# A split-precision matmul stream with high and low activations in one 512-column matmul

## The reference

```
proj = h @ w_in                      # 7 blocks of 128 columns a head: 3 q, 3 k, 1 v
g = g * sigmoid(g @ w_gate);  mix = g @ w_out        # state-space layer
a = h @ w_up
a = conv_b + sum(conv_w[j] * shifted(a, j))          # along time, width 3
ffn = (silu(gate) * up) @ w_down
x = x + g1 * mix;   x = x + g2 * ffn
```

## Time and profile before

| | |
|---|---|
| median of three runs | 2,897.93 us |
| the profiled execution | 2,893.69 us |
| its span, first to last instruction | 2,891.9 us |
| PE busy / DVE busy / ACT busy | 2,787.8 / 2,165.3 / 1,233.9 us |
| mean granted TensorE clock | 0.987 |
| mean DMA rate | 251 GB/s |

### The profile page before, as it was taken

One profiled execution on the slowest core, in us unless ns is written; L12 is line 12 of the kernel. 1 busy time (PEld: TensorE's weight loads), 2 busy tenths in 40 slices (PEclk: granted clock), 3 DMA queues, 4 the chain that ended last, 5 costly groups with the idle time before them and its releaser, 6 DMA issues.

```text
span 2891.9 us, 59942 instructions
## 1 busy us (share of the span) xinstructions
PE 2787.8 (96%) x23900; PEld 2730.2 (94%) x23900; DVE 2165.3 (75%) x2765; ACT 1233.9 (43%) x1687; POOL 458.6 (16%) x469
## 2 busy tenths in 40 slices
PE   8799999999989999999999999989989999999998
PEld 3789999999989999999999998989989999999998
DVE  7877766667759988889888778987688654566654
ACT  1434444444433544434444334444354443444532
POOL 4051101011024011000110121234311110011111
PEclk9999999999999999999999999999999999999999
DMA  9889877778757788778888877868868666665663
GB/s 360 344 288 372 287 256 256 253 252 269 253 162 258 281 298 286 266 230 300 298 297 304 270 245 217 240 216 300 283 216 300 184 176 185 187 183 183 180 182 110
DMA packets 241712, 724.83 MB, mean 251 GB/s; under 512 B 50912, under 2 KB 59872, under 8 KB 240736
## 3 DMA queue, kind: packets, MB, share of 16 engines
q1 hardware_dynamic: 185184, 666.98, 68.7%
q10 hardware_dynamic: 56320, 54.93, 6.1%
HBM read 700.58 MB, written 25.43 MB: 251 GB/s over the span
## 4 chain that ended last, share of the span: by engine, by line
PE 87%; DVE 6%; DMA 3%; issue 2%; ACT 1%; POOL 1%; ACTq 1%; SPq 0%; DVEq 0%; POOLq 0%
PE proj L1749 27%; PE proj L1750 27%; PE proj L1751 27%; DVE acc L986 2%; PE pmisc L1773 1%; DMA raw<-in_w_in 1%; DMA ada<-in_ada_w 1%; PE ps L1828 1%; DVE w_lo L1077 1%; PE ps L1855 1%; PE proj L1828 1%; PE ps L1939 1%; DVE work L1039 0%; ACT w_hi L547 0%; ACTq L615 0%
## 5 line engine op out<-in xcount | busy, mean ns | idle before, releaser
L1077 DVE TENSOR_TENSOR w_lo<-raw,w_hi 128x1024 fp32r<-128x1024 f32 (+1 forms) x896 | 1112.4, 1243 | 609.8 <-ACT w_hi L547 604.3
L547 ACT ACTIVATE w_hi<-raw 128x1024 fp32r<-128x1024 f32 (+1 forms) x896 | 933.8, 1045 | 1423.6 <-PE proj L1751 1322.7
L1749 PE MATMUL proj<-h_hi,w_hi 128*128 128x256 f32 x5120 | 1471.8, 287 | 47.2 <-DVE h_lo L1032 13.2
L1750 PE MATMUL proj<-h_lo,w_hi 128*128 128x256 f32 x5120 | 1456.7, 285 | 0.0
L1751 PE MATMUL proj<-h_hi,w_lo 128*128 128x256 f32 x5120 | 1456.3, 284 | 0.0
L1749 PEld LDWEIGHTS proj<-h_hi,w_hi 128*128 128x128 f32 x5120 | 988.4, 193 | 59.4 <-issue 20.7
L1750 PEld LDWEIGHTS proj<-h_lo,w_hi 128*128 128x128 f32 x5120 | 990.0, 193 | 0.0
L1751 PEld LDWEIGHTS proj<-h_hi,w_lo 128*128 128x128 f32 x5120 | 989.5, 193 | 0.0
L1749 PE MATMUL proj<-a_hi,w_hi 128*128 128x256 f32 x1920 | 547.2, 285 | 10.0 <-DVE x L1381 6.6
L1750 PE MATMUL proj<-a_lo,w_hi 128*128 128x256 f32 x1920 | 545.7, 284 | 0.0
L1751 PE MATMUL proj<-a_hi,w_lo 128*128 128x256 f32 x1920 | 545.6, 284 | 0.0
(11 more groups left out here) (237 smaller groups left out, 1516.3 us busy)
## 6 DMA issues: line engine op xcount, KB each, us to landing
raw<-in_w_up SPq DMA_DIRECT2D x352, 512.0 KB, 5.7
ada<-in_ada_w SPq DMA_DIRECT2D x348, 512.0 KB, 5.5
raw<-in_w_in SPq DMA_DIRECT2D x224, 512.0 KB, 5.6
raw<-in_w_down SPq DMA_DIRECT2D x128, 448.0 KB, 3.8
raw<-in_w_down SPq DMA_DIRECT2D x64, 512.0 KB, 3.7
raw<-in_w_out SPq DMA_DIRECT2D x32, 512.0 KB, 4.7
raw<-in_ssm_w_in SPq DMA_DIRECT2D x32, 512.0 KB, 4.6
raw<-in_ssm_w_gate SPq DMA_DIRECT2D x32, 512.0 KB, 5.8
```

Source lines behind the costliest of these rows:

```text
L547: nc.scalar.activation(w_hi[:, j % LAG, 0:nk * P], raw[:, j % s.ring, 0:nk * P], ACT.Copy).then_inc(hi_ready, 1)
L1077: V.tensor_tensor(w_lo[:, j % LAG, 0:nk * P], raw[:, j % s.ring, 0:nk * P], w_hi[:, j % LAG, 0:nk * P].bitcast(F32), ALU.subtract).then_in ...
L1749: mm(o, w_hi[:, j % LAG, w], hi[:, k, :], start=(k == (k0 if held else 0)), stop=False)
L1750: mm(o, w_hi[:, j % LAG, w], lo[:, k, :], start=False, stop=False)
```

## The change

Nine streams are marked wide: qkv1, qkv, ssm_out and all of layer 1's feed-forward part. In them the moving operand of the high weights is the high and the low activations side by side, 512 columns; the bank's first half takes high x high (and, as before, low x high), its second half high x low. The high and low activations become one tensor with two halves. Who takes a block out adds the second half to the first:

- heads: ACT copies the second half to SBUF, and DVE adds the first half to it (`gather`, due with the copy);
- into the residual stream: DVE does its multiply and add twice, first for the second half, and waits in between for its own result;
- up-projections: ACT copies the second half to `whole` (`tail`), DVE adds the first (`join_halves`) and frees the bank; the taps read `whole`, one step later.

In a block's last k step the low weights come before the wide matmul. The stream up1a is now one pass of 20 blocks in place of two of 12, up1a_end has 24 blocks in place of 20, and the ada parts taken there are spread over both.

```
+WIDE = {"qkv1", "qkv", "ssm_out", "up1a", "up1a_end", "down1a", "up1b", "up1b_end", "down1b"}
-    add("up1a", 2, 12, two, ada=(1, 10, spread(16, 20, 4)), sum_due=24, take_due=27)
-    add("up1a_end", 1, 20, two)
+    add("up1a", 1, 20, two, ada=(1, 10, spread(16, 36)))
+    add("up1a_end", 1, 24, two, ada=(1, 11, spread(16, 36, 4)), sum_due=44, take_due=47)
...
-        a_hi, a_lo = sb("a_hi", [HALF, T], F32R), sb("a_lo", [HALF, T], F32R)
-        h_hi, h_lo = sb("h_hi", [KT, T], F32R), sb("h_lo", [KT, T], F32R)
+        a_hl, h_hl = sb("a_hl", [2, HALF, T], F32R), sb("h_hl", [2, KT, T], F32R)
+        a_hi, a_lo, h_hi, h_lo = a_hl[:, 0], a_hl[:, 1], h_hl[:, 0], h_hl[:, 1]
...
+                    if s.wide:
+                        nc.scalar.activation(dst, proj[(7 * hl + m) % 2][:, T:2 * T], ACT.Copy).then_inc(q_tail, 1)
+                        return
                     nc.scalar.activation(dst, proj[(7 * hl + m) % 2][:, 0:T], ACT.Copy).then_inc(block_out, 1)
...
+                def tail(pl, side):
+                    def f(i):
+                        pair = pair0 + i * (s.blocks // 2) + pl
+                        block_ready(s, i, 2 * pl + side)
+                        wait(act, conv2, 2 * (pair - first_wide_pair) + side - 1)
+                        nc.scalar.activation(whole[:, side, :], proj[side][:, T:2 * T], ACT.Copy).then_inc(up_tail, 1)
+                    return f
...
+                    for side in range(2) if s.wide else ():
+                        late.setdefault(4 * pl + 5 + 2 * side, []).append(tail(pl, side))
+                    late.setdefault(4 * pl + 5 + s.wide, []).append(tap2(pl, 0))
+                    late.setdefault(4 * pl + 7 + s.wide, []).append(tap2(pl, 1))
...
+            def gather(s, i0, hl, m):
+                def f(i):
+                    b = 7 * hl + m
+                    dst = v_t if m == 6 else qk[:, hl, m, :]
+                    dve.wait_ge(q_tail, 14 * (i + i0 - 1) + b + 1)
+                    V.tensor_tensor(dst, proj[b % 2][:, 0:T], dst, ALU.add).then_inc(block_out, 1)
+                return f
...
+                    for m in range(7) if s.wide else ():
+                        late.setdefault(14 * hl + 2 * m + 5, []).append(gather(s, i0, hl, m))
                     late.setdefault(14 * hl + 14 + 7, []).append(softmax(i0, hl))
...
+                        if s.wide:
+                            V.scalar_tensor_tensor(out=x[:, k, :], in0=proj[b % 2][:, T:2 * T], scalar=g, in1=x[:, k, :],
+                                                   op0=ALU.mult, op1=ALU.add).then_inc(tail_added, 1)
+                            dve.wait_ge(tail_added, tails_before(name) + k + 1)
                         V.scalar_tensor_tensor(out=x[:, k, :], in0=proj[b % 2][:, 0:T], scalar=g, in1=x[:, k, :],
                                                op0=ALU.mult, op1=ALU.add).then_inc(block_out, 1)
...
+                def join_halves(pl, side):
+                    def f(i):
+                        pair = pair0 + i * (s.blocks // 2) + pl
+                        dve.wait_ge(up_tail, 2 * (pair - first_wide_pair) + side + 1)
+                        V.tensor_tensor(whole[:, side, :], proj[side][:, 0:T], whole[:, side, :], ALU.add
+                                        ).then_inc(block_out, 1)
+                    return f
...
+                        if s.wide:
+                            late.setdefault(4 * pl + 5 + 2 * side, []).append(join_halves(pl, side))
+                        late.setdefault(4 * pl + 5 + 2 * side + s.wide, []).append(taps10(pl, side))
...
+                    both = proj[b % 2][:, :].rearrange("p (c t) -> p c t", c=2)
+                    hl = a_hl if hi is a_hi else h_hl
...
+                        end = last and k == k0 + nk - 1
+                        if s.wide:
+                            if end:
+                                mm(o, w_lo[:, j % LAG, w], hi[:, k, :], start=False, stop=False)
+                            ins = mm(both, w_hi[:, j % LAG, w], hl[:, :, k, :], start=(k == 0), stop=end)
+                            if not end:
+                                ins = mm(o, w_lo[:, j % LAG, w], hi[:, k, :], start=False, stop=False)
+                            continue
                         mm(o, w_hi[:, j % LAG, w], hi[:, k, :], start=(k == (k0 if held else 0)), stop=False)
                         mm(o, w_hi[:, j % LAG, w], lo[:, k, :], start=False, stop=False)
```

More of the change, by code:

```diff
@@ L56 @@
 ADA = 4
+WIDE = {"qkv1", "qkv", "ssm_out", "up1a", "up1a_end", "down1a", "up1b", "up1b_end",
+        "down1b"}
 CHUNK = 4
@@ L67, in __init__ @@
         self.name, self.ring, self.tight, self.slots, self.ada = name, ring, tight, slots, ada
+        self.wide = name in WIDE
         self.length = len(pieces)
@@ L276, in build @@
         conv, o = cut(work, 2400, 2, 2, T)
+        whole, _ = cut(work, 5472, 2, T)
         silu, o = cut(work, o, 2, T)
@@ L392, in build, with tails_before @@
         UPS = {"up0a": 0, "up0a_end": 18, "up0b": 22, "up0b_end": 40,
-               "up1a": 44, "up1a_end": 56, "up1b": 66, "up1b_end": 86}
+               "up1a": 44, "up1a_end": 54, "up1b": 66, "up1b_end": 86}
+        first_wide_pair = min([UPS[n] for n in UPS if n in WIDE])
+        def tails_before(name):
+            n = 0
+            for s in st.values():
+                if s.name == name:
+                    return n
+                if s.wide and not s.name.startswith(("up", "qkv")):
+                    n += s.count * s.blocks
         def ada_part_done(name):
@@ L785, in f @@
                         fb = f0 + i * (s.blocks // 2) + pl
-                        block_ready(s, i, 2 * pl + side)
+                        if s.wide:
+                            act.wait_ge(block_out, s.block(i, 2 * pl + side) + 1)
+                        else:
+                            block_ready(s, i, 2 * pl + side)
                         wait(act, gated_ready, pair - 1)
-                        nc.scalar.activation(conv[:, pl % 2, side, :], proj[side][:, 0:T], ACT.Identity,
+                        nc.scalar.activation(conv[:, pl % 2, side, :], whole[:, side, :] if s.wide else proj[side][:, 0:T],
+                                             ACT.Identity,
                                              bias=tap_b[:, fb, side:side + 1],
@@ L791, in f @@
                         if side == 1:
-                            act.wait_ge(block_out, s.block(i, 2 * pl) + 1)
+                            if s.wide:
+                                act.wait_ge(conv2, 2 * (pair - first_wide_pair) + 1)
+                            else:
+                                act.wait_ge(block_out, s.block(i, 2 * pl) + 1)
                             nc.scalar.activation(silu[:, pl % 2, :], conv[:, pl % 2, 0, :], ACT.Silu).then_inc(silu_ready, 1)
@@ L1413, in f @@
                         dve.wait_ge(conv0, 2 * pair + side + 1)
-                        V.scalar_tensor_tensor(out=cv[:, 1:T], in0=proj[side][:, 0:T - 1], scalar=tap(1), in1=cv[:, 1:T],
+                        src, made = (whole[:, side], conv2) if s.wide else (proj[side], block_out)
+                        V.scalar_tensor_tensor(out=cv[:, 1:T], in0=src[:, 0:T - 1], scalar=tap(1), in1=cv[:, 1:T],
                                                op0=ALU.mult, op1=ALU.add).then_inc(conv1, 1)
                         dve.wait_ge(conv1, 2 * pair + side + 1)
-                        V.scalar_tensor_tensor(out=cv[:, 2:T], in0=proj[side][:, 0:T - 2], scalar=tap(0), in1=cv[:, 2:T],
-                                               op0=ALU.mult, op1=ALU.add).then_inc(block_out, 1)
+                        V.scalar_tensor_tensor(out=cv[:, 2:T], in0=src[:, 0:T - 2], scalar=tap(0), in1=cv[:, 2:T],
+                                               op0=ALU.mult, op1=ALU.add).then_inc(made, 1)
                         if side == 1:
-                            dve.wait_ge(block_out, s.block(i, 2 * pl + 1) + 1)
+                            if s.wide:
+                                dve.wait_ge(conv2, 2 * (pair - first_wide_pair) + 2)
+                            else:
+                                dve.wait_ge(block_out, s.block(i, 2 * pl + 1) + 1)
                             dve.wait_ge(silu_ready, pair + 1)
@@ L1426, in up @@
                     for side in range(2):
-                        late.setdefault(4 * pl + 5 + 2 * side, []).append(taps10(pl, side))
+                        if s.wide:
+                            late.setdefault(4 * pl + 5 + 2 * side, []).append(join_halves(pl, side))
+                        late.setdefault(4 * pl + 5 + 2 * side + s.wide, []).append(taps10(pl, side))
                 take_parts(s, late)
@@ L1748, in piece @@
                         w = slice((k - k0) * P, (k - k0 + 1) * P)
+                        end = last and k == k0 + nk - 1
+                        if s.wide:
+                            if end:
[4 more added lines that the diff above has]
+                            continue
```

(2 more changed lines are left out.)

8 lines of the change are left out of this document (4 added, 4 removed).

## The result

| | before | after |
|---|---|---|
| median of four runs | 2,899.23 us (2,894.52 to 2,902.14) | 2,873.57 us (2,867.78 to 2,876.29) |
| span of the profiled execution | 2,891.9 us | 2,873.1 us |
| mean granted TensorE clock | 0.987 | 0.985 |

The ratio is 0.9911, 95% interval 0.9895 to 0.9926: 26 us faster. The forecast was 86 us faster and a range of 2,790 to 2,858 us; the time lies above it. The sign was right, the size was not.

What follows compares the result with a forecast made beforehand. PE's matmul stream was taken as the bound, its pitch set by the next weights' load. Terms -94.5 + 1.3 + 3.5 + 3.4 + 0.5 + 1 - 1 = -85.8 gave 2,807.9, forecast 2,812 us, range 2,790 to 2,858.

Steps and rivals of the forecast that it cites:

- the term of PE: Wide streams: one weight load of three goes, a k step takes 0.336 instead of 0.360 us; 94.5 us saved.
- extra time goes with every matmul: Rival, wide streams: 13 ns belong to each change of weights, a step takes 347 ns; 2,856 us, chance 0.13.
- The reading of the earlier trace: Steady matmul stream: the next weights' load, about 120 ns and not following the array's clock, sets the 256-column pitch.
- K steps, instruction counts: Wide streams: 3,936 k steps, each with three 256-column matmuls becoming one of 512 and one of 256.
- The additions: Evacuations: DVE busy +23 us (residual stream), +41 (gathers), +37 (up-projection additions), mostly hidden behind PE.
- half clock: Wide streams: nothing saved at half clock, where about 20 us of wide work stand; +1.3 us.
- PE's wait where the probabilities are turned: Heads: the gather behind ACT's delayed evacuation adds 0.5 us once a pass, +3.5 us over 7 passes.
- behind the softmax: Heads: the gather behind the softmax on DVE fits by 0.3 us; cost 0, up to 1 us a head.
- In qkv1: Stage qkv1, with DMA share 0.98: only 2 of its 5.4 us on PE come through; +3.4 us.
- The plan of up1a: Layer 1 up-projections: +1 us where late banks do not fit, -1 us from ada adds spread over 36 steps twice.
- The wait for L1417: up1a: PE's one wait of 1.7 us should shrink as ada adds are spread; -1 us.
- The stream itself is slow: Rival, wide streams: operands enter at 0.47 ns a column, 512 columns take 240 ns; 2,907 us, slower, chance 0.07.

Runs made afterwards that it cites:

- the widths: Changed kernel with each layer 1 feed-forward stream given its own width for both matmuls of a k step, products partly left out; 2,826.64 us in one run.
- the types: Changed kernel with up1b on constant bf16 operands and down1b in plain float32, up1b's product left out; 3,187.13 us in one run.
- in pairs: Changed kernel with ACT's probabilities copy behind the evacuation and each second k step turned round (512, 256, 256, 512); 2,850.95 us, ratio 0.9837 against before.

## Why the prediction was wrong

**The step that failed** is the term of PE, "The 512-column matmul streams 213 ns and hides the load behind it: I take 0.216 us (half of the f32 pitch, rounded up)". It measures 227 among its like and 233 to 241 in the alternation. The forecast's 336 ns a step became 352.6, which is 16.6 x 3,936 = 65 us of the 60 that the forecast was off; the other terms gave 5 back.

- Some 11 of the 16.6 ns (42 us) are the fixed 13.3 ns, shown by the widths and the types. This was the rival "extra time goes with every matmul", to which I gave 0.13. What I held against it did not bear on it: the f32 row is of a type with 2.5 ns, and at half clock no width shows the 13 ns. The one-column matmuls at 111 missed the 120 that I put down to the load by 9 ns, and I passed over the 9.
- The reading of the earlier trace rows, that something which does not follow the array's clock sets the 120, was wrong about the load: with 128 columns the pitch is 213 ns at half clock, so the pace that I took for the load's goes with the clock. The row of 256 columns could not tell it from the stream.
- The other 6 ns (23 us) are mostly the slow rhythm, of which neither forecast nor rival spoke. With it the time lies at 2,874, not at the rival's 2,856.
- **K steps, instruction counts:** right, 3,936 matmuls fewer.
- **The additions:** DVE's busy time grew by 85 us, where the forecast had 101; the cost on PE's path was 4 us, the plan's gain within it (forecast 8.7 with 1.3 of half clock; at 0.64 us a step the 20 us at half clock hold 31 wide steps, so that term should have been 0.8). The durations of DVE's instructions grew by 98 us; the busy time grew less because they overlap a little. PE's wait where the probabilities are turned grew from 0.93 to 1.39 us, forecast +0.5; behind the softmax, where the forecast had 0 to 1 us a head, PE waits nowhere in the six passes of qkv. In qkv1 stage and saving together give 2.6 us, forecast 3.4.
- **The plan of up1a:** nothing measurable, as forecast. The wait for L1417 of the earlier trace rows went.
- **"The stream itself is slow"** (512 = 0.240): the single pitches of 236 to 241 look like it, but the low matmul behind it is down to 113 and 512s among themselves take 227. It is not the stream.

## What to carry to other kernels

A pitch that is the stream plus a small rest has two readings, a hidden floor and a cost of each instruction, and they part by the whole rest when instructions are merged; a row of another operand type does not choose between them, a second width of the same type does. Merging two matmuls into one wider saved here one fixed cost of 13.3 ns at the most: 7.4 ns a step in strict alternation, 11.7 in pairs (360 to 348.3). Where wide and narrow matmuls alternate, try the order of pairs: it cost nothing here and gave 13 us. A row in which two limits come to the same number, as the 213 ns at half clock, tells nothing of either; take a second width.

## What was not expected of the hardware

- At full clock reduced float32 matmuls of one width follow each other at columns / 2.4 GHz + 13.3 ns (256 to 512 columns), bf16 at + 2.5 ns, plain float32 at twice the columns + 2.5 ns.
- At half clock reduced float32 matmuls of 128 and 256 columns are both 213 ns apart and those of 512 columns 427, with nothing added; at full clock the shortest pitch was 110 to 113 ns.
- One sequence of 512 and 256 columns runs at 347 or at 353 ns a pair, with the same instructions from one execution to the next on one chip, and keeps to one for up to hundreds of microseconds. Between two executions of one kernel, on two chips, the streams that changed took 6.8 us more; its runs lay between 2,863.55 and 2,878.84 us, at mean granted clocks of 0.981 to 0.986, so not all of this is rhythm.
- With 96 or 64 columns of weights the 512-column pitch was 230 ns, longer than the 227 with 128.
